# Reordering the split weights and the last operand parts at the start of each down phase, and shifting operand and weight addresses of two stages

## The reference

```
def swiglu(x, w_in, w_out):                      # stages f0, f1
    gate, up = jnp.split(x @ w_in, 2, axis=-1)
    return (jax.nn.silu(gate) * up) @ w_out

def conv_glu_ffn(h, w_up, conv_w, conv_b, w_down):   # stages g0, g1
    u = causal_dwconv(jnp.einsum('btd,df->btf', h, w_up), conv_w, conv_b)
    gate, val = jnp.split(u, 2, axis=-1)
    return jnp.einsum('btf,fd->btd', jax.nn.silu(gate) * val, w_down)
```

## Time and profile before

| | |
|---|---|
| device time, three runs | 2563.66 us median (2562.94 to 2565.49) |
| profiled execution | 2568.07 us, its span 2566.3 us |
| PE busy | 2520.3 us, 98% of the span |
| DVE, ACT busy | 1622.9 us, 1163.3 us |
| share of the chain that ended last | PE 88%, DVE 6%, ACT 3%, DMA 2% |
| PE idle until a low part of weights came, at down units | 11.4 us, 10 times |

### The profile page before, as it was taken

The page is one execution under the profiler, slowest core; times in us unless marked ns, Lnnn a source line. Parts: engine busy times, 40 slices in busy tenths (PEclk is TensorE's granted clock), DMA queues, the critical chain, the costliest instruction groups (busy, mean ns, idle before and its releaser), DMA issues.

```text
span 2566.3 us, 44717 instructions
## 1 busy us (share of the span) xinstructions
PE 2520.3 (98%) x19246; PEld 2296.5 (89%) x19246; DVE 1622.9 (63%) x2784; ACT 1163.3 (45%) x1924; POOL 169.4 (7%) x219
## 2 busy tenths in 40 slices
PE   9999999999999999999999999999999999999998
PEld 7777889889877888989899899999999989999998
DVE  5767756457566665546766557666675754766666
ACT  4554533335455443334554435434444534544443
POOL 0000200100000110110000011001000000200100
PEclk9999999999999999999999999999999999999999
DMA  5222955974322593895311249259652122954975
GB/s 192 89 66 70 255 150 162 294 193 147 103 82 65 158 248 97 268 256 164 140 67 51 69 160 259 84 174 287 157 187 93 65 71 97 263 143 141 291 175 163
DMA packets 104311, 397.33 MB, mean 155 GB/s; under 512 B 10416, under 2 KB 12720, under 8 KB 84272
## 3 DMA queue, kind: packets, MB, share of 16 engines
q1 hardware_dynamic: 60400, 249.07, 28.5%
q0 software_dynamic: 42992, 143.82, 23.9%
q10 hardware_dynamic: 720, 1.57, 0.2%
HBM read 383.80 MB, written 133.30 MB: 201 GB/s over the span
## 4 chain that ended last, share of the span: by engine, by line
PE 88%; DVE 6%; ACT 3%; DMA 2%; issue 1%; SPq 0%; POOL 0%; DVEq 0%; ACTq 0%; POOLq 0%
PE P L756 59%; PE P L1090 13%; PE P L854 3%; PE P L877 3%; PE P L763 2%; DVE WL L2193 2%; ACT WH L1551 1%; PE P L889 1%; DMA raw<-in_wts 1%; PE P L1188 1%; PE P L1209 1%; PE P L1302 1%; PE P L903 1%; PE P L935 1%; DVE X L2289 0%
## 5 line engine op out<-in xcount | busy, mean ns | idle before, releaser
L756 PE MATMUL P<-XH,WL 128*128 128x256 f32 (+3 forms) x3080 | 839.9, 322 | 15.1 <-DVE XL L2525 6.9
L756 PE MATMUL P<-XL,WH 128*128 128x256 f32 (+3 forms) x3080 | 817.0, 314 | 0.0
L756 PE MATMUL P<-XH,WH 128*128 128x256 f32 (+3 forms) x3080 | 816.7, 314 | 0.0
L2193 DVE TENSOR_TENSOR WL<-raw,WH 128x1024 fp32r<-128x1024 f32 (+2 forms) x533 | 573.9, 1079 | 317.7 <-ACT WH L1551 316.1
L1551 ACT ACTIVATE WH<-raw 128x1024 fp32r<-128x1024 f32 (+2 forms) x533 | 498.0, 941 | 465.9 <-PE P L756 223.4
L756 PEld LDWEIGHTS P<-XH,WL 128*128 128x128 f32 x3080 | 517.9, 189 | 61.2 <-DVE XL L2525 9.8
L756 PEld LDWEIGHTS P<-XH,WH 128*128 128x128 f32 x3080 | 516.3, 189 | 35.5
L756 PEld LDWEIGHTS P<-XL,WH 128*128 128x128 f32 x3080 | 515.8, 189 | 33.0
L1090 PE MATMUL P<-GHH,WL 128*128 128x272 f32 (+1 forms) x616 | 178.3, 290 | 9.5 <-DVE WL L2193 9.5
L1090 PE MATMUL P<-GHH,WH 128*128 128x272 f32 (+1 forms) x616 | 177.0, 287 | 0.0
L1090 PE MATMUL P<-GHL,WH 128*128 128x272 f32 (+1 forms) x616 | 177.0, 287 | 0.0
(11 more groups left out here) (373 smaller groups left out, 3789.8 us busy)
## 6 DMA issues: line engine op xcount, KB each, us to landing
raw<-in_wts SPq DMA_DIRECT2D x151, 1024.0 KB, 5.0
sums<-in_quads POOLq DMA_DIRECT2D x32, 1152.0 KB, 28.5
sums<-in_quads POOLq DMA_DIRECT2D x32, 960.0 KB, 24.6
sums<-in_quads POOLq DMA_DIRECT2D x16, 1536.0 KB, 19.6
raw<-sums SPq DMA_DIRECT2D x64, 384.0 KB, 3.4
sums<-in_quads POOLq DMA_DIRECT2D x16, 1280.0 KB, 13.6
raw<-sums SPq DMA_DIRECT2D x64, 320.0 KB, 3.1
raw<-in_wts SPq DMA_DIRECT2D x48, 384.0 KB, 3.6
```

Of the source, the lines that this page charges most:

```text
L756: ins = nc.tensor.matmul(P[:, a:a + x1 - x0], weight(u, wb, k), xb[:, kx, x0 - c0:x1 - c0], start=start and i == 0, stop=stop and i == 2, ...
L2193: nc.vector.tensor_tensor(weight_rows(u, WL), raw_rows(u), weight_rows(u, WH).bitcast(F), ALU.subtract).then_inc(*dve.up("wlo", u))
```

## The change

The change has five parts. (1) At the last up unit of each group (n = 23 and 43, `next_down`) ACT makes the high parts of W3 and W4 ahead of the last pair's part b, and that of W5 ahead of part t. (2) DVE there works in the order of the new function `enter_down`. (3) In g the low part of W2 goes ahead of the tile's product. (4) The table load of phase B goes behind the high part of W6. (5) `GHH` and `GHL` get rooms of 1920 numbers for each pair (7680 bytes, before 7616). In g1 the operands follow each other at 256 numbers, and in g0 still at 272, where the weights of each unit are shifted by 64 bytes times `OPERAND[p] % 4`.

```
@@ weight_places
+    for ph in range(2):
+        for n, (p, mp) in enumerate(products(ph)):
+            put(f"g0{'AB'[ph]}", n, "plain", LINE // 4 * (OPERAND[p] % 4))
@@ build
-        GHH = sb("GHH", [128, 6, 7, 272], R, ph)
-        GHL = sb("GHL", [128, 6, 7, 272], R, ph)
+        GHH = sb("GHH", [128, 6, 1920], R, ph)
+        GHL = sb("GHL", [128, 6, 1920], R, ph)
         def combined(st, xb, j, i, n=1):
             w = 272 if st == 2 else 256
-            return xb[st][:, pair_slot(j), i, 0:w] if n == 1 else xb[st][:, pair_slot(j), i:i + n, 0:w]
+            rows = xb[st][:, pair_slot(j), :, :] if st < 2 else xb[st][:, pair_slot(j), 0:7 * w].rearrange("p (i t) -> p i t", t=w)
+            return rows[:, i, :] if n == 1 else rows[:, i:i + n, :]
+        def next_down(U, n):
+            return up_unit(U, n) + 1 if n in (2 * UP_TILES[0][1] - 1, 2 * NF - 1) else None
@@ ACT: down_and_norm and down_and_sums (phase B)
-                nc.scalar.preload_act_table_set("natural_log_exp_and_others")
                 for i in range(24):
                     highs(U + i + NS)
+                    if i == 3:
+                        nc.scalar.preload_act_table_set("natural_log_exp_and_others")
@@ ACT
-            def high_parts(s, m, g, ready):
+            def high_parts(s, m, g, ready, D=None):
                 st, j = s // 2, m // 2
+                if D:
+                    highs(D + 4)
                 act.wait_ge(*at(*ready))
...
                     nc.scalar.activation(combined(st, CH, j, 2, 2), both_halves(s, g), ACT.Copy
                                          ).then_inc(*act.up("ch", s, j, "b"))
+                    if D:
+                        highs(D + 5)
                     act.wait_ge(*at("comb", s, j, "t"))
@@ DVE
+            def enter_down(s, m, D, ready):
+                st, ph = s // 2, int(m + 1 == NF)
+                lows(D + 3)
+                low_parts(s, m, "b")
+                lows(D + 4)
+                evict(st, ph, 0)
+                differences(s, m, ready)
+                lows(D + 5)
+                low_parts(s, m, "t")
+                lows(D + 6)
@@ DVE: down, down_and_norm, down_and_sums
-                    evict(st, 0, i)
+                    if i:
+                        evict(st, 0, i)
                     lows(first[STAGES[st] + "A"] + i + NS)
@@ DVE: feed_forward (f)
-                    if n % 2:
+                    if next_down(U, n):
+                        enter_down(s, m, next_down(U, n), ("mul", l, m))
+                    elif n % 2:
                         differences(s, m, ("mul", l, m))
                         low_parts(s, m)
@@ DVE: conv_glu (g)
+                    if next_down(U, n):
+                        lows(up_unit(U, n) + NS)
                     if j:
                         g = conv_buffer(m, 0)[:, a1:]
...
                     lows(up_unit(U, n) + NS)
-                    if j:
+                    if next_down(U, n):
+                        enter_down(s, m, next_down(U, n), ("gmul", l, m))
+                    elif j:
                         differences(s, m, ("gmul", l, m))
                         low_parts(s, m)
```

More of the change, by code:

```diff
@@ L1789, in feed_forward @@
                     if n % 2:
-                        high_parts(s, m, tmp[m % 4][:, 0:512], ("mul", l, m))
+                        high_parts(s, m, tmp[m % 4][:, 0:512], ("mul", l, m), next_down(U, n))
                 down_and_norm(l)
@@ L2147, in conv_glu @@
                     else:
-                        high_parts(s, m, conv_buffer(m, 0)[:, a1:], ("gmul", l, m))
+                        high_parts(s, m, conv_buffer(m, 0)[:, a1:], ("gmul", l, m), next_down(U, n))
                 down_and_sums(2 + l)
@@ L2366, in layer_norm, with low_parts @@
                         split(s, m - 2, 1)
-            def low_parts(s, m):
+            def low_parts(s, m, only="anbt"):
                 st, j = s // 2, m // 2
                 for part, i, n in (("a", 0, 1), ("n", 1, 1)) if m % 2 == 0 else (("b", 2, 2), ("t", 4, 3)):
+                    if part not in only:
+                        continue
                     dve.wait_ge(*at("ch", s, j, part))
@@ L2457, in down_and_norm @@
                 for i in range(24):
-                    evict(st, 1, i)
+                    if i:
+                        evict(st, 1, i)
                     lows(U + i + NS)
```

## The result

The changed kernel takes 2549.74 us (median of 4 runs, 2548.55 to 2550.77) where the kernel before takes 2564.4 in the same comparison (2562.94 to 2565.49): a ratio of 0.9943, 95% interval 0.9926 to 0.996. It is 14.7 us faster. I had predicted 24.6 us, and the time lies 1.7 us above my range. The direction and the removed stalls were right. Two terms of the sum were not, and the execution that all terms were read from lay above the median.

The account below looks back on a forecast made before the run. PE, busy 98% of the span, was taken as the bound. Gains of 2.0 (f), 10.0 (g's stalls), 5.0 (clock), 4.4 (g1) and 3.7 (g0), less 0.5, made 24.6 us: 2563.66 to 2539.1 us, range 2534 to 2544.

Parts of the forecast that it names:

- The order: Starts of down phases: the new ACT and DVE order removes the stall before unit 3; W6 0.13 us late next.
- The wait at the end of g1A: End of g1A: once as fast as f, it waits for the next up unit's weights, -0.5 us.
- 0.07 more in the first two [units], which is what f does: Starts of down phases: PE takes 1.70 us a unit and 0.07 more in the first two.
- 0.14 of the excess is PE's slow start, which stays: Starts of f's phases: 0.14 us of the window's excess to unit 3 remains after the change.
- f's term of 2.0 us: f's down phases: shorter starts gain 0.1 us in each phase A and 0.9 in each B, 2.0 in all.
- g1 has exactly f's places: g1's down matmuls: with f's places the pace goes from 117.2 to 112.4 ns, 4.4 us over 924 matmuls.
- I take 3.7, nearer to f's: g0's down matmuls, 272 columns: a constant distance from operand to weights gains 3.7 us, within bounds of 0 and 5.0.
- The clock, 5.0 us: Starts of g0A, g0B and g1B: without stalls of 2 us the three half-clock stretches go, 5.0 us.
- the line that my rival drew between 1.9 and 2.0 us: PE waits near the clock's limit could add or take a slow stretch, 1.7 us either way; counted within the forecast's 0.66.
- The rule of the two ports: Rival, g's down matmuls: independent ports make places irrelevant, pace stays at 118 and 125 ns; 2545.8 us, chance 0.13.
- The moved stall: Rival, phases A: slower handoffs stall PE 2 us at unit 6 or 7; 2548.5 us, chance 0.15.
- the slower case: Rival, the eight starts: part t and W6 come so late that the kernel ends 5.1 us slower; chance 0.03.

Follow-up runs that it names:

- kick_g0: Changed kernel plus one additional matmul ahead of g0's down phases, 64 columns wide in A and 96 in B: 2552.24 us, one run.
- kick_f: Changed kernel plus one additional 192-column matmul ahead of the first down matmul of all four phases of f: 2544.68 us, ratio 0.9921.
- the sweeps: Two kernels, the changed kernel with down weights of f and g shifted to other distances from their operands: 2557.18 and 2556.89 us, one run each.
- f_old_order: Changed kernel with f's two layers back in the old order of ACT and DVE: 2546.83 us, ratio 0.9927.
- kick1: Changed kernel plus one additional matmul ahead of each phase of f, 64, 128, 32 and 192 columns in f0A, f0B, f1A, f1B: 2544.37 us, one run.
- kick2: Changed kernel plus additional matmuls ahead of f's phases: two of 64 columns in f0A, 256 in f0B, 96 in f1A, 160 in f1B: 2549.82 us, one run.
- places_only: Kernel before with only the new places of operands and weights, old order of ACT and DVE: 2561.76 us, ratio 0.9985.
- order_only: Changed kernel without the new places, so only the new order of ACT and DVE: 2552.48 us, ratio 0.9947.
- sweep1: Changed kernel with down weights of f and g shifted by further multiples of 64 bytes, to distances of 128, 192 or 0: 2557.18 us, one run.

## Why the prediction was wrong

**The order, right.** The handoffs came out within 0.07 us of the reckoning, and no start stalls before unit 3. The wait at the end of g1A came as well (0.4 us).

**"0.07 more in the first two [units], which is what f does", and "0.14 of the excess is PE's slow start, which stays": the step that failed.** Units 0 and 1 of f before ran 0.07 us each over mid-phase, 15 matmuls at 118 instead of 113. I took it for a start-up effect that ends by itself. It was the other pace, and it had lasted until the stall before unit 3. Removing the stall removed its end. f's term of 2.0 us gained became 3.1 us lost (f0A +1.41, f0B and f1B +0.84 each, f1A +0.02), a miss of 5.1 us (6.5 had f1A stayed at 118 as in kick_g0). kick_f, with the same order and the other state, has f's phases 2.3 us below before (1.9 with the four additional matmuls), where I said 2.0. The term was right but for the state.

**"g1 has exactly f's places" and so f's pace: right in the trace, with luck in it.** g1's share came to 11.0 us (from 118.1 us in both phases to 107.1) where my terms add up to 11.1. The pace is f's better state, and I had no reason to expect it there rather than the other. Outside the sweeps g1B ran at it in all eight traces with the new places. g1A began with it in all eight and fell to 118 in f_old_order, kick1, kick2 and places_only, for 1.4 us each in the first three, whose g1A is the changed kernel's, instruction for instruction. I had called the pace a property of the places. It is a possibility that the places open, and no other distance of the sweeps showed it.

**"I take 3.7, nearer to f's": mis-sized.** Between starts g0's pace fell from 125.3 to 123.5 ns (my 124.5, 30 us over a count of 241, was 0.8 too low), 1.6 us for 924 matmuls, and 1.5 by the lengths of order_only and after. That is 2.1 or 2.2 us less than the term. Nothing showed that 272 columns behave as 256 do, and they don't: neither a distance nor an additional matmul took them below 123.

**The clock, 5.0 us: right in sum, but not for this comparison.** The three slow stretches at the starts of g0A, g0B and g1B are gone. Elsewhere, ahead of its last microseconds, the profiled execution of before had 10.2 us at half clock (from 1242.94, 1263.42 and 1915.37), and that of the changed kernel 10.2 too (all of PE's work, columns as above):

```profile
1905.99:1912.82 6.83, 6.10 (x21) 0.50 0.74 295
1264.28:1267.70 3.42, 3.42 (x18) 0.50 0.30 128
```

They come with waits of PE of 1.9 us (until 1906.72) and 2.7 us (until 1263.36). The same places, with waits of 1.65, 2.66 and 1.93 us (to 0.01 us the same in all three traces), had a slow stretch each in before, the last two in the changed kernel, and none in order_only:

```profile
1246.00:1249.40 3.40, 3.31 (x19) 1.00 0.00 0
1264.10:1267.50 3.40, 3.40 (x28) 1.00 0.56 239
1906.60:1910.00 3.40, 3.35 (x20) 1.00 0.73 231
```

And places_only, with stalls as long as before's, had the slow stretch in g0B and g1A but none behind those of g0A and g1B:

```profile
1676.50:1679.90 3.40, 3.40 (x29) 1.00 0.88 264
1847.91:1851.32 3.41, 3.29 (x14) 0.51 0.61 155
2329.15:2332.56 3.41, 3.41 (x19) 0.50 0.88 255
2500.00:2503.40 3.40, 3.40 (x32) 1.00 0.89 282
```

So one wait lowers the clock in one execution and not in another, and the line that my rival drew between 1.9 and 2.0 us isn't there: 1.65 lowered it, 2.72 (g1B of places_only) didn't. The profiled execution of before had three of four, six ahead of its last microseconds, and was 3.7 us slower than its median (2568.07 against 2564.4), while that of after was 1.0 us above its own. I had taken the losses of an execution that lay above the median off the median. The gain between the profiled executions is 17.3 us: 24.6 less 5.1 (f) and 2.2 (g0) is 17.3. The remaining 2.6 us to the median's 14.7 is that difference of the executions. That it is the clock's is likely and not shown for these, but it fits the 13 executions of before in the comparison of order_only: the shortest, 2559.74 us, had a mean clock of 0.999, the two longest, 2568.86 and 2568.93, 0.995 and 0.996.

**The rule of the two ports.** My rival was that places don't matter, by the Trainium skill, "TensorE: Matmul & The Clock Gate", section "Step-by-step: what each phase is for". The measurement decides against my reading of it, that places don't matter. Between order_only and the changed kernel only places differ, and g1 went from 118.1 and 118.3 ns to 113.3. Shifting f0A's weights by 64 bytes more (sweep1) gave 119 ns, where 113 and 118 were its paces. Why the places of operand and weights matter when they come through ports that the Trainium skill calls independent, no run here shows.

The moved stall and the slower case didn't come: no wait of over 0.2 us is left at the down matmuls.

## What to carry to other kernels

When a stall is removed, look at the pace of what runs before and behind it, not only at the idle time. Here it differed by 4%, and the faster one began behind the stall. A small excess at the beginning of a stretch is worth a look at its single instructions before it is called start-up. And terms taken from one profiled execution are to be weighed by where that execution lies among the runs, above all those that the clock decides.

## What the hardware showed that I had not expected

- Two steady paces of the same stream of weight load and matmul (128 x 256, fp32r) at the same addresses, 113.3 and 117.8 ns, each held for hundreds of matmuls without a drift.
- An additional matmul of 192 columns, which moves the next start by 0.09 us, took f from the slower to the faster in 9 of 9 phases, for 1.9 us in a phase of 504 matmuls; 64, 64 + 64 and 96 columns did so too, 32, 128, 160 and 256 didn't, in one phase each. Why these widths, stays open.
- A pause of 0.2 us amid a phase can end in either pace: the same f1A left it at 113 in the changed kernel and at 118 in kick_g0.
- Of eight distances (modulo 256) from operand to weights only 64 bytes showed the faster pace; 0, 32, 48, 80, 96, 128 and 192 gave 117 to 120 ns.
- With 272 columns the pace depends on the distance too (123.5 ns at 64, 124.1 at 96, 126 to 127 at 32, 128 and 192), and no second one was seen. Why, stays open.
